# The last two weight blocks of a product into x taken tile by tile, with half of the next transposes among them, and four weight roundings moved ahead of a norm's root at an FFN's entry

## What is computed

```
for i in range(2):                                     # stack 1
    x = x + 0.5 * swiglu(rmsnorm(x, ffn1_norm[i]), ffn1_w_gate[i], ffn1_w_up[i], ffn1_w_down[i])
    ... deltanet and hyena groups of rmsnorm(x, mix_norm[i]) @ w_in[i] ...
    x = x + concat([o_dn, o_hy]) @ w_out[i]
    x = x + 0.5 * swiglu(rmsnorm(x, ffn2_norm[i]), ffn2_w_gate[i], ffn2_w_up[i], ffn2_w_down[i])
x = rmsnorm(x, final_norm)
for l in range(2):                                     # stack 2
    x = x + y @ w_out_2[l]                             # y: attention, retention and convolution, gated
    gu = rmsnorm(x, norm_ffn_g_2[l]) @ w_ffn_in_2[l]
    x = x + (silu(causal_dwconv(g)) * u) @ w_ffn_out_2[l]
```

## Time and profile before

| what | value |
|---|---|
| median of 3 runs | 2306.14 us (2305.7 to 2306.58) |
| profiled execution | 2312.43 us |
| its span, first to last instruction | 2310.6 us |
| PE busy | 2164.1 us, 94% |
| POOL busy | 1521.4 us, 66% |
| ACT busy | 1015.8 us, 44% |
| DVE busy | 998.8 us, 43% |
| TensorE clock granted, mean | 0.965 |

### The profile page before, as it was taken

How to read it: one execution, slowest core, us unless ns; L and a number is a source line. 1 busy time by engine, 2 the same in 40 slices (tenths; PEclk the granted TensorE clock), 3 DMA queues, 4 the chain that set the end, 5 groups by cost and what they waited for, 6 DMA issues and landing times.

```text
span 2310.6 us, 39314 instructions
## 1 busy us (share of the span) xinstructions
PE 2164.1 (94%) x14719; PEld 1960.5 (85%) x14719; DVE 998.8 (43%) x1727; ACT 1015.8 (44%) x1458; POOL 1521.4 (66%) x664
## 2 busy tenths in 40 slices
PE   6999998989999999998989996999899989998999
PEld 6997768979988997768979986989799878897997
DVE  3451365433413551365433503263577124445760
ACT  4443426444444443426444443436444444454442
POOL 5787434527886787434527885757588866576896
PEclk9999998999999999998999998999999999999999
DMA  6655223014554655223015554534455544353553
GB/s 210 219 176 180 81 85 110 1 56 162 175 193 154 219 175 179 82 83 110 1 56 163 176 202 151 164 116 154 150 165 183 192 151 155 115 168 128 179 183 131
DMA packets 250736, 331.19 MB, mean 143 GB/s; under 512 B 9024, under 2 KB 224938, under 8 KB 250026
## 3 DMA queue, kind: packets, MB, share of 16 engines
q1 hardware_dynamic: 250074, 326.19, 42.8%
q0 software_dynamic: 464, 2.37, 0.3%
HBM read 327.48 MB, written 1.05 MB: 142 GB/s over the span
## 4 chain that ended last, share of the span: by engine, by line
POOL 41%; issue 32%; PE 22%; DVE 2%; ACT 2%; POOLq 0%; DMA 0%; ACTq 0%; DVEq 0%
POOL w_lo L855 39%; PE psA L397 3%; PE psB L397 3%; PE psB L399 3%; PE psB L398 3%; PE psA L399 3%; PE psA L398 3%; PE psA L1595 2%; PE psB L1618 1%; PE psB L1625 1%; POOL Mm_even L847 1%; POOL Mm_odd L847 1%; PE psA L1584 1%; PE psA L1710 1%; POOLq L854 0%
## 5 line engine op out<-in xcount | busy, mean ns | idle before, releaser
L855 POOL TENSOR_TENSOR w_lo<-raw,w_hi 128x1024 fp32r<-128x1024 f32 x600 | 1452.0, 2439 | 721.7 <-ACT w_hi L545 721.0
L397 PE MATMUL psA<-xT_hi,w_lo 128*128 128x256 f32 x3296 | 957.5, 290 | 49.3 <-POOL w_lo L855 19.8
L398 PE MATMUL psA<-xT_lo,w_hi 128*128 128x256 f32 x3296 | 943.4, 286 | 0.0
L399 PE MATMUL psA<-xT_hi,w_hi 128*128 128x256 f32 x3296 | 943.4, 286 | 0.0
L545 ACT ACTIVATE w_hi<-raw 128x1024 fp32r<-128x1024 f32 x600 | 629.0, 1051 | 389.0 <-PE psB L399 234.0
L397 PEld LDWEIGHTS psA<-xT_hi,w_lo 128*128 128x128 f32 x3296 | 643.5, 195 | 62.9 <-issue 27.0
L398 PEld LDWEIGHTS psA<-xT_lo,w_hi 128*128 128x128 f32 x3296 | 643.7, 195 | 2.9 <-issue 2.9
L399 PEld LDWEIGHTS psA<-xT_hi,w_hi 128*128 128x128 f32 x3296 | 643.0, 195 | 0.0
L978 DVE TENSOR_TENSOR hT_lo<-hfull,hT_hi 128x256 fp32r<-128x256 f32 x132 | 239.1, 1844 | 7.8 <-ACT hT_hi L602 7.1
L397 PE MATMUL psB<-w_hi,hT_lo 128*128 128x512 f32 x528 | 209.2, 396 | 0.5 <-POOL w_lo L855 0.5
L398 PE MATMUL psB<-w_lo,hT_hi 128*128 128x512 f32 x528 | 209.0, 396 | 0.0
(11 more groups left out here) (372 smaller groups left out, 2362.1 us busy)
## 6 DMA issues: line engine op xcount, KB each, us to landing
raw<-in_w_in SPq DMA_DIRECT2D x78, 1024.0 KB, 5.1
raw<-in_ffn_w_gate SPq DMA_DIRECT2D x44, 1024.0 KB, 5.1
raw<-in_ffn_w_up SPq DMA_DIRECT2D x44, 1024.0 KB, 5.2
raw<-in_ffn_w_down SPq DMA_DIRECT2D x44, 1024.0 KB, 4.8
raw<-in_w_ffn_in SPq DMA_DIRECT2D x44, 1024.0 KB, 5.0
raw<-in_w_ffn_out SPq DMA_DIRECT2D x22, 1024.0 KB, 4.7
raw<-in_w_out SPq DMA_DIRECT2D x16, 1024.0 KB, 4.8
raw<-in_w_branch_da SPq DMA_DIRECT2D x4, 1024.0 KB, 4.7
```

The source lines that it names most:

```text
L397: nc.tensor.matmul(o, a_lo, b_hi, start=start, stop=False, skip_group_check=skip)
L398: nc.tensor.matmul(o, a_hi, b_lo, start=False, stop=False, skip_group_check=skip)
L399: return nc.tensor.matmul(o, a_hi, b_hi, start=False, stop=stop, skip_group_check=skip)
L855: nc.gpsimd.tensor_tensor(split_half(w_lo, n, kind), raw_half(n, kind), split_half(w_hi, n, kind).bitcast(F32), ALU.subtract)\
```

## The change

It has three parts.

1. `into_x` with `last` or whole: the last two blocks are no longer done one after the other over all four tiles. PE waits for both blocks' weights, then does both blocks for tile (0,0), then for (0,1), (1,0) and (1,1). Where a `turned` offset is given (the product ahead of four of the FFN entries, and the product of stack 1's second FFN, in both layers), the four transposes of tile (0,0) follow tile (0,1), and those of tile (0,1) follow tile (1,0). `turn_rows` keeps the eight transposes of row block 1. The first entry's eight stand ahead of the loop.
2. ACT: the last of the three roundings ahead of an entry moves behind the roundings of xT_hi (`late`).
3. ACT: at j = 0 three roundings that stood between the Silus and the roundings of h, and a Silu of one column (which brings its table in), are put ahead of `root_across` and behind it: two ahead of it, one right behind `root_row`, and the first of j = 0 stays where it was.

```diff
-            def norm_out_gained(st, l, q, x0):
+            def norm_out_gained(st, l, q, x0, late):
                 square_rows(st, l, x0, 0)
...
                     ins_.then_inc(n_hi[st].sem, 1)
+                round_half(st, l, late)
                 square_rows(st, l, x0, 1)
...
-                        round_half(st, l, s0 + 4 * j + i + AHEAD)
+                        if j:
+                            round_half(st, l, s0 + 4 * j + i + AHEAD)
                         if n == 0:
+                            round_half(st, l, s0 + AHEAD)
+                            A(stat[:, 47:48], eps, ACT.Silu)
+                            round_half(st, l, s0 + 1 + AHEAD)
+                            round_half(st, l, s0 + 2 + AHEAD)
                             root_across(st, l, f)
                             act.wait_ge(root_mm[st].sem, root_mm[st].due(l, f + 1))
                             A(root_row[:, :], psB[:, 0, 0:L], ACT.Copy).then_inc(root_out[st].sem, 1)
+                            round_half(st, l, s0 + 3 + AHEAD)
...
-                        round_half(st, l, s0 + 4 * j + 2 + i + AHEAD)
+                        if j:
+                            round_half(st, l, s0 + 4 * j + 2 + i + AHEAD)
...
+                final = len(blocks) - 2 if whole or last else len(blocks)
...
+                for rb in range(RB):
+                    for c in range(2):
+                        for n, k in enumerate(blocks):
+                            if n >= final:
+                                ins_ = accumulate(n, k, rb, c, False, n == len(blocks) - 1)
+                                if rb == 1 and c == 1:
+                                    ins_.then_inc(half_used[st].sem, 1)
+                        if rb == 0 or c == 0:
+                            ins_.then_inc(rows_done[st].sem, 1)
+                        if turned is not None and (rb, c) == (0, 1):
+                            turn_block(st, l, 0, 0, turned)
+                        if turned is not None and (rb, c) == (1, 0):
+                            turn_block(st, l, 0, 1, turned)
```

More of the change, by code:

```diff
@@ L718, in stack1_mixer @@
                     A(xT_hi[:, 2 * p:2 * p + 2, :], oy[:, 2 * p:2 * p + 2, :], ACT.Copy).then_inc(s1["y_hi"].sem, 1)
-                for k in range(4, 8):
+                for k in range(4, 7):
                     round_half(0, l, 94 + k + AHEAD)
@@ L794, in stack2_mixer @@
                     A(yT_hi[:, n, :], yacc[:, n, :], ACT.Copy).then_inc(s2["yb_hi"].sem, 1)
-                for k in range(8):
+                for k in range(7):
                     round_half(1, l, 58 + k + AHEAD)
@@ L799, in _ @@
             with act.Fori(0, DEPTH) as l:
-                for n in range(AHEAD):
+                for n in range(AHEAD - 1):
                     round_half(0, l, n)
-                norm_out_gained(0, l, 0, -4)
+                norm_out_gained(0, l, 0, -4, AHEAD - 1)
                 ffn(0, l, 0, 0)
@@ L805, in _ @@
                 stack1_mixer(l)
-                norm_out_gained(0, l, 2, 4)
+                norm_out_gained(0, l, 2, 4, 101 + AHEAD)
                 ffn(0, l, 1, 102)
@@ L815, in _ @@
                 stack2_mixer(l)
-                norm_out_gained(1, l, 1, 0)
+                norm_out_gained(1, l, 1, 0, 65 + AHEAD)
                 ffn(1, l, 0, 66)
@@ L1478, in turn_x, with turn_block, turn_rows @@
                     ins_.then_inc(n_tp[st].sem, 1)
[L1480 to L1489, removed]
+            def turn_block(st, l, rb, c, x0):
+                pe.wait_ge(x_ready[st].sem, x_ready[st].due(l, x0 + 2 * rb + c + 1))
+                for kc in range(4 * c, 4 * c + 4):
+                    v = (kc % 2) * L + rb * P
+                    ins_ = nc.tensor.transpose(psA[:, kc // 2, v:v + P], x[:, rb, kc * P:(kc + 1) * P], ident)
+                    if rb == RB - 1 and kc % 2:
+                        ins_.then_inc(n_tp[st].sem, 1)
+            def turn_rows(st, l, x0):
+                turn_block(st, l, 1, 0, x0)
+                turn_block(st, l, 1, 1, x0)
             def root_across(st, l, f):
@@ L1518, in project_two, with into_x, block_ready @@
                 ins_.then_inc(half_used[st].sem, 2)
-            def into_x(st, l, s0, a_hi, a_lo, made=None, counted=0, blocks=None, last=False):
+            def into_x(st, l, s0, a_hi, a_lo, made=None, counted=0, blocks=None, last=False, turned=None):
                 whole = blocks is None
-                blocks = range(a_hi.shape[1]) if whole else blocks
-                for n, k in enumerate(blocks):
+                blocks = list(range(a_hi.shape[1]) if whole else blocks)
+                final = len(blocks) - 2 if whole or last else len(blocks)
+                def block_ready(n, k):
                     pe.wait_ge(lo_done[st].sem, lo_done[st].due(l, s0 + n + 1))
@@ L1528, in into_x, with accumulate @@
                         pe.wait_ge(made.sem, made.due(l, counted + k + 1))
+                def accumulate(n, k, rb, c, starts, ends):
+                    t, v = slice(rb * P, (rb + 1) * P), slice(c * 512, (c + 1) * 512)
                     hi, lo = split_half(w_hi, s0 + n, "B"), split_half(w_lo, s0 + n, "B")
-                    starts = n == 0 and (whole or s0 == 94)
-                    ends = n == len(blocks) - 1 and (whole or last)
+                    return product(psB[:, 2 * rb + c, :], a_hi[:, k, t], a_lo[:, k, t], hi[:, v], lo[:, v], starts, ends)
+                for n, k in enumerate(blocks[:final]):
+                    block_ready(n, k)
                     for rb in range(RB):
-                        t = slice(rb * P, (rb + 1) * P)
                         for c in range(2):
[L1535 to L1538, removed]
+                            ins_ = accumulate(n, k, rb, c, n == 0 and (whole or s0 == 94), False)
                     ins_.then_inc(half_used[st].sem, 1)
+                if final == len(blocks):
+                    return
+                for n, k in enumerate(blocks):
+                    if n >= final:
+                        block_ready(n, k)
+                for rb in range(RB):
+                    for c in range(2):
+                        for n, k in enumerate(blocks):
+                            if n >= final:
+                                ins_ = accumulate(n, k, rb, c, False, n == len(blocks) - 1)
[7 more added lines that the diff above has]
+                            turn_block(st, l, 0, 1, turned)
             def ffn(st, l, f, s0, q):
@@ L1560, in ffn @@
                     pe.wait_ge(s1["mlp_arg"].sem, s1["mlp_arg"].due(l, 3))
-                into_x(st, l, s0 + 2 * NF, hT_hi, hT_lo, f_lo[st], NF * f)
+                into_x(st, l, s0 + 2 * NF, hT_hi, hT_lo, f_lo[st], NF * f, turned=8 if st == 0 and f == 1 else None)
             def turn_rows1(l):
@@ L1799, in deltanet @@
                 pe.wait_ge(s1["y_lo"].sem, s1["y_lo"].due(l, 6))
-                into_x(0, l, 100, xT_hi, xT_lo, blocks=(2, 3), last=True)
+                into_x(0, l, 100, xT_hi, xT_lo, blocks=(2, 3), last=True, turned=4)
             def scores(l, k):
@@ L1933, in stack2_mixer @@
                 pe.wait_ge(s2["br"].sem, s2["br"].due(l, 20))
-                into_x(1, l, 58, yT_hi, yT_lo, s2["yb_lo"])
+                into_x(1, l, 58, yT_hi, yT_lo, s2["yb_lo"], turned=0)
             pe.sem_inc(half_used[0].sem, SLOTS)
@@ L1941, in _ @@
             nc.tensor.transpose(psB[:, 1, 0:7 * KC], rows[0:7 * KC, :], ident[0:7 * KC, 0:7 * KC]).then_inc(gain_turned, 1)
+            turn_block(0, 0, 0, 0, -4)
+            turn_block(0, 0, 0, 1, -4)
             with pe.Fori(0, DEPTH) as l:
-                turn_rows(0, l, 0, -4)
+                turn_rows(0, l, -4)
                 ffn(0, l, 0, 0, 0)
@@ L1948, in _ @@
                 deltanet(l)
-                turn_rows(0, l, 2, 4)
+                turn_rows(0, l, 4)
                 ffn(0, l, 1, 102, 2)
@@ L1953, in _ @@
                 stack2_mixer(l)
-                turn_rows(1, l, 1, 0)
+                turn_rows(1, l, 0)
                 ffn(1, l, 0, 66, 1)
```

## The result

The changed kernel takes 2324.66 us (median of 4 runs, 2323.43 to 2325.76), the kernel before 2306.03 us. The ratio is 1.0088, 95% interval 1.0075 to 1.0100: 18.6 us slower. The forecast was 2322.

What follows compares the result with a forecast made beforehand. PE, busy 94% of the span, sets the pace. Root waits +12.2, transposes +1.9, first entry -1.0 and clock +3.5 sum to +16.6 us; 2306.1 + 16.4 = 2322.5, said as 2322. Own range 2314 to 2330; 8 in 10, 2296 to 2332.

Steps and rivals of the forecast that it cites:

- The bound and the two waits per entry: PE sets the pace; each FFN entry waits at the restart and for the fifth half's w_lo, the latter 17.9 us in all.
- rival (a): The root's chain gets through beside POOL, so the waits and the clock's 10 us go: 2279 us; chance 0.14.
- The holds: Root's chain beside busy POOL: four of 14 DVE instructions each last until a half ends; root ready at 531.5, not 524.9.
- the first entry: The first FFN entry: one rounding ahead of its xT_hi, 1.0 us, -1.0 in the sum; its root wait 4.0 us.
- The entries that differ: Root waits at the layer's first FFN, 3.5 us, and at the first entry, 4.0 us, against 5.6 or 5.7 elsewhere.
- The clock: Slow clock after PE's waits at the six entries: 14 us against 10 now, +3.5; 0 to +8 at its ends.
- The transposes at four entries: Part 1's tiles and transposes at four entries: ACT's first xT_hi starts at the same time, so they give nothing.
- root waits: PE's waits for the root at six entries: 30.1 us, less the 17.9 us of now, +12.2.
- the loop's restart: Restart after the loop's end: 0.95 us later, with DVE's last add; wait grows from 2.8 to between 3.2 and 3.7 us.
- 0.95 ahead of stack 2: Final norm ahead of stack 2: the same eight transposes for nothing, another 0.95 us.
- the sign: Change makes the kernel slower; slower by more than 4.6 us has 0.68, within it 0.12, faster 0.20.

Runs made afterwards that it cites:

- The kernel with part 3 and a quick root: Kernel before with ACT's order at j = 0 as changed, and POOL waiting for the root ahead of an entry's second half: 2273.8 us, ratio 0.9881.
- POOL's wait: POOL begins an entry's second half only when the root is ready; added to the changed kernel 2285.9 us, alone in the kernel before 2303.5 us.
- the second trace of the kernel before: The kernel before run once more, no edit, for another trace: 2302.9 us, ratio 0.9989.

## Why the prediction was right

**The bound and the two waits per entry** were read rightly. The kernel with part 3 and a quick root has neither, and is 1.2% faster than before (27 us by the ratio). That is the size at which rival (a) was priced, though it needed POOL's wait, which the change does not have.

**The holds** were the step on which all hung, and they came as counted: at the mixer entries L876, L878, L880 and L884 of the changed kernel (L868, L870, L872 and L876 in the prediction's numbers) each last until a half of POOL's ends, L881 slips through behind L880, and the rest take 0.16 us. The wait was priced at 5.6 and 5.7 us and is 5.15: counted from PE's restart, the root is ready 0.2 us sooner than I had it, the turning starts 0.3 us sooner, and PE comes to it 0.2 us later. The rule of the Trainium skill (page "SBUF — State Buffer", section "SBUF: two separate sides"), that a DVE instruction with two SBUF inputs or in a two-port mode and a GpSimd one exclude each other, agrees with the traces here for the chain's instructions with two SBUF inputs (L884 here, L888 at the first entry). Three of the four that were held have one SBUF input (L876, L878, L880); they fall under the rule's other case, a two-port mode, if they ran in one, which no trace here shows. What it leaves open, who is next, they show: at each end of a half DVE gets one instruction (2.33, 2.32 and 2.18 us in the changed kernel), or two where the second does not wait for the first. A short gap lets more through: at the first entry 0.34 us between two halves passed three.

**The entries that differ** were sized worse. At the first I had 4.0 us and it is 2.87, with four held as well. In the loop I had 0.95 us more of restart and then 3.5 us for the root. It is 3.3 us more for the restart (0.89 and 5.20 against 2.77) and no wait for the root: after the long wait PE ran its first weight halves at a granted 0.63, ACT's rounding of half 4 had to wait for that, and the chain found POOL idle after its second half. Windows of the changed kernel, columns as in the earlier trace rows, at the loop's entry, at the first mixer's entry and at the first entry of all:

```profile
720.70:728.00 7.30, 7.30 (x41) 7.30 (x42) 4.97 (x20) 2.67 (x4) 3.57 (x3) 0.63 0.41 128
...
530.10:537.00 6.90, 6.89 (x40) 6.89 (x41) 2.06 (x6) 2.94 (x7) 2.38 (x1) 0.65 0.32 110
...
34.90:40.00 5.10, 5.07 (x42) 5.07 (x43) 2.51 (x6) 3.26 (x7) 2.41 (x1) 1.00 0.55 185
```

**The clock** was priced at 14 us against 10. By each stretch's length times the part not granted, the six entries of the changed kernel lose 2.7, 2.4, 2.8, 2.5, 1.6 and 0 us, 12.0, against 10.5 in the second trace of the kernel before and 11.3 in the first.

**The transposes at four entries** give nothing, as priced. The restart after the mixers waits 0.71 us instead of 1.28, with 0.35 us of waiting in front of the last eight transposes. From the start of the product's first block to the restart it is 15.88 us after the first mixer, against 15.81.

**Costed at nothing, and not nothing:** the first of the four tiles now needs the weights of both last blocks at its start. In stack 2 POOL is not that far ahead, and PE waits 0.76 and 0.75 us there, once in each layer, which no row of the kernel before has.

In the sum: root waits 23.5 against 17.9, +5.6 (I had +12.2); the loop's restart +3.3 and 0.95 ahead of stack 2 (I had 1.9 for the two); the two waits for the last blocks' weights +1.5; the first entry -1.1 (-1.0); clock +1.5 by the second trace of the kernel before, +0.7 by the first (+3.5). That is 11 to 11.8 us, near the 12.9 between the two spans and 7 short of the 18.6 between the medians. The forecast's 16.4 (its own terms add up to 16.6) met the median to 3 us by luck, as far as the size goes: the root term was twice too large, others were too small, and some 7 us of the measured difference are in no term. What was right by reasoning is the four holds, the wait of over 5 us that they make at four entries, and so the sign.

Where the last 7 us lie is open. The changed kernel's trace is of an execution at its median (2325.35 us) and has both mixer stretches long; that of the kernel before is 6 us above its median with both long too. If the executions at that median have one of them short, 4.6 us of the rest are explained; no trace of such an execution was taken.

## What to carry to other kernels

The short chain of tiny DVE instructions was slow here not by its work but by what POOL did beside it: count the chain's dependent SBUF instructions against POOL's instructions, one for each, before moving work for POOL ahead of it. Where both are needed, let POOL wait for the chain (2.6 us at the mixer entry) rather than the chain for POOL (10.2 us from its first instruction to the root, 2.6 without POOL). Alone, a quick chain is worth nothing where PE waits for something else behind it. And a DVE instruction far longer than others of its shape can be a wait in the disguise of busy time; look whether one of POOL's ended when it did.

## What the runs showed of the hardware that was not expected

- DVE's first instruction behind the branch of stack 1's loop comes 2.3 to 2.7 us after its last one in five traces, and 4.8 to 5.7 us in three with eight transposes on PE at the loop's end (3.9 in a fourth), although ACT had written the first xT_hi before. Taking these transposes out brought it back to 2.66 us. That they cause it is shown; how they do is open.
- After a wait of 5.15 us PE ran at a granted 0.60 to 0.77 for the next 7 us, but at 1.00 after 2.87 us at the first entry, and at about 0.6 after 2.7 us in the kernel before. The length of the wait alone does not say what the clock will do.
